# A depthwise convolution as 31 rounds of sixteen 32x32 matmuls, and a new order of the chunks around it

## What is computed

```python
q, k, v, ca, cg = jnp.split(u @ w_in[i], SPLITS, axis=-1)      # 512, 128, 128, 512, 512 columns
attn = _sliding_window_attention(rope(q), rope(k), v, sinks[i])
conv = _conformer_conv(ca, cg, conv_w[i], ...)                 # below
mixed = concat([rms_norm(attn), rms_norm(conv)])
h = h + mixed @ w_out[i]

def _conformer_conv(a, g, w_dw, b_dw, ln_g, ln_b):
    u = a * sigmoid(g)
    y = depthwise_conv(u, w_dw) + b_dw       # 31 causal taps, each of 512 channels by itself
    return silu(layer_norm(y, ln_g, ln_b))
```

## Time and profile before

| | |
|---|---|
| median of three runs | 1580.86 us (1579.62 to 1581.09) |
| the profiled execution's own time | 1578.84 us |
| its span, first to last instruction | 1577.2 us |
| PE busy | 1485.0 us, 94% |
| DVE busy | 926.0 us, 59% |
| ACT busy | 795.8 us, 50% |
| mean granted clock of PE | 0.977 |
| HBM read | 247.77 MB, 158 GB/s |

### The profile page before, as it was taken

One profiled execution on the slowest core, in us unless ns is written; L12 is line 12 of the kernel. 1 busy time (PEld: TensorE's weight loads), 2 busy tenths in 40 slices (PEclk: granted clock), 3 DMA queues, 4 the chain that ended last, 5 costly groups with the idle time before them and its releaser, 6 DMA issues.

```text
span 1577.2 us, 20618 instructions
## 1 busy us (share of the span) xinstructions
PE 1485.0 (94%) x6985; PEld 1223.8 (78%) x6985; DVE 926.0 (59%) x1279; ACT 795.8 (50%) x1204; POOL 14.0 (1%) x29
## 2 busy tenths in 40 slices
PE   6987889999999999999799999989999997999996
PEld 5875668888887888888688888768888886888884
DVE  4675655665555555658565555565565676655545
ACT  5665654555445444454364444464444544644434
POOL 2000000000000000000000000000000000000000
PEclk9998999999999999999899999989999998999998
DMA  8752324565665665652056655556656511666541
GB/s 216 219 214 72 89 67 133 175 201 172 183 192 184 203 184 179 186 169 89 27 185 187 182 179 161 181 161 186 185 175 186 175 41 54 202 186 186 180 149 46
DMA packets 132775, 249.95 MB, mean 158 GB/s; under 512 B 8736, under 2 KB 16352, under 8 KB 132688
## 3 DMA queue, kind: packets, MB, share of 16 engines
q1 hardware_dynamic: 130256, 244.91, 50.6%
q0 software_dynamic: 1360, 3.70, 1.4%
q10 hardware_dynamic: 1072, 0.24, 0.1%
HBM read 247.77 MB, written 1.05 MB: 158 GB/s over the span
## 4 chain that ended last, share of the span: by engine, by line
PE 87%; ACT 5%; DVE 4%; issue 2%; ACTq 1%; DMA 0%; DVEq 0%
PE acc L1786 25%; PE acc L1787 25%; PE acc L1788 25%; PE turn L1799 4%; PE score L2074 3%; ACT w_hi L634 2%; DVE w_lo L1118 1%; PE score L1822 1%; ACT xs L646 1%; DVE y L1608 1%; PE score L2149 1%; PE outp L2111 1%; DVE xc L1331 1%; PE score L1824 1%; PE outp L1840 1%
## 5 line engine op out<-in xcount | busy, mean ns | idle before, releaser
L1118 DVE TENSOR_TENSOR w_lo<-stage,w_hi 128x1024 fp32r<-128x1024 f32 (+2 forms) x480 | 562.5, 1185 | 412.5 <-ACT w_hi L634 402.3
L634 ACT ACTIVATE w_hi<-stage 128x1024 fp32r<-128x1024 f32 (+2 forms) x480 | 486.7, 1028 | 497.3 <-PE acc L1788 494.1
L1786 PE MATMUL acc<-w_hi,x_hi 128*128 128x512 f32 (+2 forms) x1296 | 516.0, 398 | 21.7 <-DVE x_lo L1174 11.3
L1787 PE MATMUL acc<-w_lo,x_hi 128*128 128x512 f32 (+2 forms) x1296 | 505.1, 390 | 0.0
L1788 PE MATMUL acc<-w_hi,x_lo 128*128 128x512 f32 (+2 forms) x1296 | 504.7, 389 | 0.0
L1786 PEld LDWEIGHTS acc<-w_hi,x_hi 128*128 128x128 f32 x1296 | 247.0, 191 | 73.9 <-DVE w_lo L1118 22.6
L1788 PEld LDWEIGHTS acc<-w_hi,x_lo 128*128 128x128 f32 x1296 | 246.4, 190 | 51.4
L1787 PEld LDWEIGHTS acc<-w_lo,x_hi 128*128 128x128 f32 x1296 | 247.1, 191 | 46.8
L1786 PE MATMUL acc<-w_hi,g_hi 128*128 128x512 f32 x352 | 138.0, 392 | 0.0
L1788 PE MATMUL acc<-w_hi,g_lo 128*128 128x512 f32 x352 | 137.2, 390 | 0.0
L1787 PE MATMUL acc<-w_lo,g_hi 128*128 128x512 f32 x352 | 137.1, 390 | 0.0
(11 more groups left out here) (317 smaller groups left out, 1208.3 us busy)
## 6 DMA issues: line engine op xcount, KB each, us to landing
stage<-in_ffn_w_gate_up SPq DMA_DIRECT2D x176, 512.0 KB, 3.7
stage<-in_ffn_w_down SPq DMA_DIRECT2D x88, 512.0 KB, 4.1
stage<-in_w_in SPq DMA_DIRECT2D x64, 512.0 KB, 4.9
stage<-in_w_ff SPq DMA_DIRECT2D x64, 512.0 KB, 4.4
stage<-in_w_out SPq DMA_DIRECT2D x16, 512.0 KB, 4.6
stage<-in_w_ple_gate SPq DMA_DIRECT2D x16, 512.0 KB, 4.4
stage<-in_w_lru_up SPq DMA_DIRECT2D x8, 512.0 KB, 3.7
stage<-in_w_o SPq DMA_DIRECT2D x8, 512.0 KB, 3.9
```

What stands on the lines that cost most here:

```text
L634: act.activation(w_hi[:, n.slot(SPLIT), 0:t, 0:w], stage[:, n.slot(STAGE), 0:t, 0:w], ACT.Copy).then_inc(hi_done, 1)
L1118: dve.tensor_tensor(w_lo[:, n.slot(SPLIT), 0:t, 0:w], stage[:, n.slot(STAGE), 0:t, 0:w], w_hi[:, n.slot(SPLIT), 0:t, 0:w].bitcast(F32), AL ...
L1786: pe.matmul(dst, xh, wh, start=kt == 0, stop=False)
L1787: pe.matmul(dst, xh, wl, start=False, stop=False)
```

## The change

The whole convolution goes to PE. A matmul with a 128x128 diagonal uses one part in 128 of its weights; here the array is used as sixteen tiles of 32x32, each with a 32x32 diagonal. `u` is written with its columns in another order, so that after the turn partition block r of column group c of `u_t` holds channels 128 r + 32 c to 128 r + 32 c + 31. Tile (r, c) reads partitions 32 r to 32 r + 31 and writes partitions 32 c to 32 c + 31 of PSUM bank r, so four banks take the four groups of `y`. A round is one tap on all sixteen tiles; 31 rounds are 496 fp32 matmuls of 32x32 weights and 256 columns for each layer.

The banks are both `acc` buffers, in two new places `Lconv0`, `Lconv1` of the plan between `Lca` and `Lout_a0`. The chunk order becomes `Lq`, `Lkv`, `Lcg`, `Lca`, and the attention's steps lie inside the matmuls of `Lcg` and `Lca`; its scores go to `pair` (the two banks that were `score` and `outp`), its results to the `turn` buffers. DVE has no taps left. ACT and DVE each move two groups of `y` out of PSUM, adding the bias. The taps' weights are loaded in the new order, by four transfers for each layer in the place of one, and the diagonals are 32 wide.

```diff
-       + [(n, U) for n in ("cg", "ca", "kv", "q")]
+       + [(n, U) for n in ("q", "kv", "cg", "ca")]
...
-TAPS_PE = 26
...
-                act.dma_start(rawt[:, l, :], a["conv_w_2"][l].rearrange("j (r p) -> (j r) p", p=P)).then_inc(s_vecs2, 16)
+                for c in range(KC):
+                    act.dma_start(rawt[c * TAPS2:(c + 1) * TAPS2, l, :].rearrange("j (r k) -> j r k", r=KC),
+                                  a["conv_w_2"][l].rearrange("j (r c k) -> c j r k", r=KC, c=KC)[c]).then_inc(s_vecs2, 16)
...
-                def taps(lo, hi):
-
-                    for j in range(lo, hi):
-                        if j == TAPS_PE:
-                            wait(dve, score_free, SCORES.at("Lconv", 1, layer))
-                        for n in range(KC - 1 if j >= TAPS_PE else KC - 2):
-                            w = tcur[:, j * KC + n:j * KC + n + 1]
...
+                    ins = dve.tensor_tensor(u[:, t, :].rearrange("p (c r k) -> p r c k", c=KC, r=KC),
+                                            acc[b][:, t, :].rearrange(quads, r=KC, c=KC),
+                                            sig[:, t, :].rearrange(quads, r=KC, c=KC), ALU.mult)
...
-                def conv(lo, hi):
-
-                    for k in range(lo, hi):
-                        i, j = (0, k) if k < TAPS_PE else (1, k - TAPS_PE)
-                        last = j == (TAPS2, TAPS_PE)[i == 0] - 1
-                        w = diag2[:, j, :] if i == 0 else diag3[:, j, :] if j < 16 else diag4[:, j - 16, :]
-                        mm = pe.matmul(score[:, i * S:(i + 1) * S], w, u_t[:, KC - 2 + i, j:j + S], start=j == 0, stop=last)
...
+                def conv():
+
+                    for j in range(TAPS2):
+                        for c in range(KC):
+                            for r in range(KC):
+                                rows_in = slice(r * QUAD, (r + 1) * QUAD)
+                                out_bank = acc[CHUNKS.at(CONVS[r // 2], 0, layer).slot(2)]
+                                mm = pe.matmul(out_bank[c * QUAD:(c + 1) * QUAD, r % 2, 0:S], diag[rows_in, c * TAPS2 + j, :],
+                                               u_t[rows_in, c, j:j + S], start=j == 0, stop=j == TAPS2 - 1)
+                    mm.then_inc(s_conv, 1)
...
+                chunk("Lkv", x_hi, x_lo, layer)
+                wait(pe, s_qk, Count(2, [(layer, 2)]))
+                turn_rows("Lq", qk2[:, :, 0:HEADS, :].rearrange("p t n d -> p t (n d)"), 2, layer)
+                pe.wait_ge(s_masks, 1)
+                wait(pe, out_free, OUTS.at("win", 8))
+                chunk("Lcg", x_hi, x_lo, layer, ready=beside_gate)
+                chunk("Lca", x_hi, x_lo, layer, ready=beside_conv_in)
+                joint_values(2)
+                evacuated(pe, "Lca", layer)
+                turn_rows("Lu", u, 2, layer)
...
+                wait(pe, s_mixo, Count(2, [(layer, 1)]))
+                turn_rows("Lmixed", mixo2, 2, layer)
+                conv()
...
-                wait(pe, s_y, Count(1, [(layer, 1)]))
-                feature_means(0, y)
...
-                    if kt == UNIT_K:
+                    if kt == 1:
+                        for name in CONVS:
+                            evacuated(pe, name, layer)
+                        feature_means(0, y)
+                    elif kt == 3:
                         wait(pe, s_ysq, Count(1, [(layer, 2)]))
                         feature_means(1, ysq)
```

More of the change, by code:

```diff
@@ L63 @@
 KC = CONV // P
+QUAD = P // KC
 WINDOW = 128
@@ L989, in _ @@
                 swiglu("a", mix_boundary, layer)
[L991 to L1010, removed]
                 def joint_exps(m):
-                    n = CHUNKS.at(JOINT[m], 0, layer)
-                    b, s = n.slot(2), m % 2
+                    s = m % 2
                     heads_in, w = (HEADS, P) if m == 0 else (HEADS // KV, S)
@@ L1058, in _ @@
                 ins.then_inc(s_sqattn, 1)
+                n = CHUNKS.at("Lconv0", 0, layer)
+                wait(act, s_conv, Count(1, [(layer, 1)]))
+                for r in range(2):
+                    ins = act.activation(y[:, r, :], acc[n.slot(2)][:, r, 0:S], ACT.Identity,
+                                         bias=vcur[:, V2["conv_b"] + r:V2["conv_b"] + r + 1])
+                ins.then_inc(acc_free[n.slot(2)], 1)
                 wait(act, score_free, SCORES.at("Lsum", 1, layer))
@@ L1680, in _ @@
+                split("Lout_a0", layer, units=range(1, 2))
                 for k in range(2):
                     turned_lo(x_hi, x_lo, "Lmixed", k, vcur[:, V2["attn"]:V2["attn"] + 4], layer)
-                taps(25, TAPS2).then_inc(s_y, 1)
+                split("Lout_a1", layer)
+                n = CHUNKS.at("Lconv1", 0, layer)
+                wait(dve, s_conv, Count(1, [(layer, 1)]))
+                for r in range(2):
+                    ins = dve.tensor_scalar(y[:, 2 + r, :], acc[n.slot(2)][:, r, 0:S],
+                                            vcur[:, V2["conv_b"] + 2 + r:V2["conv_b"] + 3 + r], None, ALU.add)
@@ L2078, in joint_scores @@
                 def joint_scores(m):
[L2080 to L2083 removed]
+                    t, per, w = (0, HEADS // 2, P) if m == 0 else (1, PAIRS // 2, S)
+                    free(SCORES, score_free, "Latt", m, layer)
                     for i in range(2):
[L2085 removed]
+                        pe.matmul(pair[:, i, :], ident_r[:, :],
@@ L2115, in _ @@
-                chunk("Lkv", x_hi, x_lo, layer, ready=conv_in)
-                chunk("Lq", x_hi, x_lo, layer)
-                turns_read(pe, "Lu", 2, layer)
-                wait(pe, s_diag, Count(1, [(layer, 1)]))
-                free(SCORES, score_free, "Lconv", 0, layer)
-                conv(0, 8)
-                wait(pe, s_kd, Count(2, [(layer, 1)]))
-                turned("Lk", 0, pieces(kd2[:, :, :, :, :].rearrange("p t b i d -> p t (b i d)"), 0), layer)
-                wait(pe, s_qk, Count(3, [(layer, 2)]))
```

294 lines of the change are left out of this document (148 added, 146 removed).

## The result

The changed kernel takes 1592.45 us (median of four runs, 1591.23 to 1593.8) beside 1580.64 us for the kernel before (1579.62 to 1581.09), a ratio of 1.0076 with an interval of 1.0058 to 1.0093. It is slower by 0.8%, where I had said 1569.8 and faster. The span of the profiled execution is 1589.6 us, 12.4 more than before.

A forecast was written before the change was run, and what follows sets the result against it. PE's own stream, busy 94% of the span, was taken as the bound. Two layers at X - 33.8 plus 2.1 once give 2 x 27.2 - 65.5 = -11.1 us, so 1569.8 us was predicted, range 1539 to 1600.

The forecast's parts named there:

- Once, in the first block: Before the layers: ACT issues six more small transfers at 0.35 us each, 2.1 us on PE's path.
- rival D: Convolution: a 32-column weight load can't lie beside a matmul of its row group; 33.9 us a layer, 1583.2 us; chance 0.14.
- waits in the attention: Attention steps beside the gate chunk: taken as 0, with up to 3 us a layer kept for the range.
- X: Time of the 496 small convolution matmuls in each layer, forecast as 27.2 us; no change at 32.8.
- keep to their lists: Convolution: each row group runs its matmuls in program order while column groups overlap; 124 x 0.217 = 26.9 us a layer.
- rival B: Convolution: all sixteen tiles run at once, 13.8 us a layer; -37.9, 1543.0 us; chance 0.22.
- Rival C: Convolution: column groups of one row group run one after another; X = 53.8, +42.1, 1623.0 us; chance 0.16.
- The wait for `y` and the half clock behind it: First mean after the convolution: PE's wait for DVE's taps, 9.8 us a layer, and slow-clock work behind it, 2.3, go.
- Behind the last tap: Between convolution and `Lout_a0`: PE waits for ACT's two copies to free the bank of `Lconv0`, about 1.1 us.
- the copy of the turned `u`: Ahead of the convolution: PE waits for one copy of the turned half and a signal, 0.7 us.
- ahead of `Lout_c0`: Path from last tap to `Lout_c0`: 17.0 us against PE's own work of 15.5, so a new wait of 1.5.
- X - 33.8: Change in us for each layer: X, less 37.1 that goes, plus 3.3 of new waits.

The follow-up runs named there:

- the loop: The changed kernel with the taps' transfers on GpSimd, rounds 2 to 30 looping over one round's 16 matmuls; 1570.46 us against 1587.57 without looping.

## Why the prediction was wrong

**The failed step** is the one headed "Once, in the first block": "six more issues are 6 x 0.35 = 2.1 us on the path". The path was right, and that PE has no slack there. The price was not: 25.1 us, twelve times as much (the wait for `w_lo` grew by 20.9, and PE restarted at the lower clock behind it). I took the row of 0.32 us as the price of an issue, but it belongs to transfers in a form with one row of 512 bytes each. The changed form costs 0.62 us to issue by itself, and its 992 pieces from 31-row transfers hold the queue until they are taken, in a stretch in which GpSimd's tables fill the engines. With this one term right and all others as predicted the sum gives 2 x 27.2 - 67.6 + 25.1 = +11.9 us, and the measured change is +11.8. That the two agree so closely is partly luck, as is that 1592 lies inside the range of 1539 to 1600: its upper part stood for rival D and for waits in the attention, and neither occurred.

**X** was right in size (26.5 for 27.2) and wrong in its reason. Row groups don't keep to their lists: all sixteen tiles run at once, as rival B had it, but without pauses the rounds take 19.8 us and not 13.8 (0.64 us each and not 0.434), and code loading adds 6.7 us to that. That the sum comes near 27.2 is luck. The Trainium skill, "TensorE: Matmul & The Clock Gate", Part 3, has sixteen tiles at once, and in that the trace agrees (starts 7 ns apart). The same page has matmuls start in the order of the program. If the two passes of a matmul stand next to each other there, the trace contradicts it, for the second pass of each tile comes behind the first pass of those after it. Rival C (slower, X = 53.8) had the right side for a reason that didn't occur; D didn't occur either.

**What held.** The wait for `y` and the half clock behind it went, and the clock is 1.00 in the convolution. Behind the last tap PE waits 1.0 us (predicted 1.1), for the copy of the turned `u` 0.8 (0.7), ahead of `Lout_c0` 1.4 (1.5). The attention beside the gate chunk costs no wait. Of the terms for a layer, X - 33.8 gives -7.3 with the measured X, and the mixers gave -6.2 and -6.0; 0.5 of the rest is a wait for `u` ahead of its turn, which I had not counted, and some 0.6 is not accounted for.

**What stays open.** Why a round of 32 passes takes 0.64 us and not 0.434; whether the DMA engines are filled as the last column of the table says, since no trace names them; and what the 31-row transfers would cost ACT without GpSimd's traffic in the first block. Replacing the prime 31 by another cut of the same weights was tried in one form only.

## What to carry to other kernels

Read the issue time of a DMA from a row of the same shape, or treat it as unknown: a row of 0.32 us says nothing of a transfer with a prime number of rows while another queue fills the DMA engines, and an engine that issues it is held with all its other work. A small reordering is cheaper on the chip, off the path, than in the pattern of a load. When many short instructions are unrolled, look for pauses named "issue" at even distances and set them against the instruction packets: work with little code placed between them hides the loading.

## What the runs showed of the hardware

- PE's instructions came in packets of 16384 bytes, one per 3.5 us or so, each good for 128 small matmul records with their loads (2.7 us of work in fp32, 1.5 in bf16 at the full clock). PE went on 1.3 to 1.6 us after a packet had landed.
- Issuing transfers of 31 x 4 x 128 bytes held ACT for up to 7.7 us apiece in the changed kernel (9.7 in the kernel before with the same transfers) and SyncE for up to 6.9, and took 0.62 on ACT at best; one of 124 x 512 bytes took 0.32. Alone, such transfers passed 107 pieces of 128 bytes per us.
- Sixteen fp32 tiles of 32x32 start 7 ns apart and, as I read the records, interleave by pass: 0.68 us a round between pauses in fp32 (0.64 in the loop) and 0.18 in bf16 at the full clock, about a quarter for half the passes.
- With pauses of 1.07 and 2.01 us between 1.5 us of bf16 matmuls the granted clock fell from 1.00 to 0.50 (1.2 GHz).
